# Memory and neighbourhood attention as one stream with dealt-out projections: a hybrid encoder block on 8 cores

## The reference

```python
h = rmsnorm(x) ; parts = h @ w_in                  # 1024 x 11264
# A: three groups of 8 heads of 64 (dilation 1, 4, 16), partial rotary,
#    each query sees keys within 64 steps of its dilated subsequence;
#    the groups are combined by their softmax denominators
# B: 8 heads of 64 on the grid of 32 rows x 64 columns: each query attends
#    8 rows x 16 columns around it (clipped at the edges), with a bias
#    per head and relative position; softmax
# C: 4 heads of 128, cross-attention into rmsnorm(mem) @ w_mem_kv
y = sum(sigmoid(logits_b + bias_b) * ((out_b * silu(g_b)) @ w_branch_b))
x = x + rmsnorm(y @ w_out)
```

## Time and profile before

| | us |
|---|---|
| median of 3 runs | 1269.59 (1269.53 to 1351.25) |
| profiled execution, device time | 1278.77 |
| its span on the slowest core (6) | 1277.2 |
| spans of the eight cores | 1254.3 to 1277.2 |
| stage 0, to A's first q projection | 75.1 |
| A | 75.1 to about 545 |
| C | about 545 to 661 |
| B | 661 to 936.6 (TensorE) |
| merge | 939 to 1206 |
| output | 1206 to 1277 |

### The profile page before, as it was taken

How to read it: one execution, slowest core, us unless ns; L and a number is a source line. 1 busy time by engine, 2 the same in 40 slices (tenths; PEclk the granted TensorE clock), 3 DMA queues, 4 the chain that set the end, 5 groups by cost and what they waited for, 6 DMA issues and landing times.

```text
span 1277.2 us, 21131 instructions; the slowest of 8 cores (1254.3 to 1277.2 us)
## 1 busy us (share of the span) xinstructions
PE 1099.4 (86%) x6768; PEld 539.1 (42%) x6768; DVE 638.6 (50%) x800; ACT 536.5 (42%) x873; POOL 399.6 (31%) x362
## 2 busy tenths in 40 slices
PE   2669999989789988569977899998959999999995
PEld 1535555444344543233344344644424444444442
DVE  3624456557684766844780089107932222222266
ACT  4515554323345432129932465246522222222365
POOL 0113333234454333343320144104532333333300
PEclk9779999989899998789988955895569999999997
DMA  9961204020017434043006410352052000400077
GB/s 228 173 128 15 37 2 51 2 34 1 1 17 68 55 45 51 1 65 78 30 1 81 67 18 2 54 77 35 2 65 34 1 1 1 66 1 1 23 256 266
DMA packets 54988, 68.13 MB, mean 53 GB/s; under 512 B 2272, under 2 KB 46432, under 8 KB 54624
## 3 DMA queue, kind: packets, MB, share of 16 engines
q0 software_dynamic: 44768, 30.41, 19.7%
q1 hardware_dynamic: 10112, 36.36, 9.3%
HBM read 86.81 MB, written 8.39 MB: 75 GB/s over the span
## 4 chain that ended last, share of the span: by engine, by line
PE 64%; DMA 11%; ACT 8%; DVE 7%; issue 7%; POOL 3%; SPq 0%; ACTq 0%; DVEq 0%; POOLq 0%
PE psall L351 26%; PE psall L485 19%; DMA xs<-x 4%; DMA ring<-w_in 3%; PE psall L671 3%; PE psall L724 3%; PE psall L955 3%; PE psall L977 3%; PE psall L544 2%; DVE t L582 2%; ACT pB L964 2%; PE psall L982 1%; DMA wbr<-w_br 1%; PE psall L1021 1%; ACT qb L534 1%
## 5 line engine op out<-in xcount | busy, mean ns | idle before, releaser
L351 PE MATMUL psall<-hT,ring 128*128 128x512 bf16 x1408 | 333.4, 387 | 22.1 <-ACT qcT L866 11.7
L485 PE MATMUL psall<-hT,ring 128*128 128x512 bf16 x896 | 225.6, 393 | 3.0 <-DMA ring<-w_in 3.0
L351 PEld LDWEIGHTS psall<-hT,ring 128*128 128x128 bf16 x1408 | 138.7, 99 | 198.5 <-issue 42.7
L1121 DVE TENSOR_TENSOR tt<-psall,sg 128x512 f32<-128x512 f32 x96 | 66.4, 692 | 202.2 <-ACT sg L1110 173.5
L1110 ACT ACTIVATE sg<-psall,mb_sb 128x512 f32<-128x512 f32 x96 | 66.0, 687 | 196.2 <-PE psall L351 196.2
L485 PEld LDWEIGHTS psall<-hT,ring 128*128 128x128 bf16 x896 | 85.0, 100 | 113.5 <-issue 33.9
L968 DVE TENSOR_TENSOR pn<-pB,ebr 128x384 bf16<-128x384 bf16 (+3 forms) x136 | 61.4, 478 | 141.1 <-ACT pB L964 124.3
L550 POOL TENSOR_TENSOR qT<-t,t 128x512 bf16<-128x512 f32 x48 | 63.6, 1325 | 163.6 <-DVE t L548 162.2
L680 ACT ACTIVATE pA<-psall 128x896 bf16<-128x896 f32 (+1 forms) x80 | 77.8, 972 | 85.5 <-PE psall L671 80.2
L964 ACT ACTIVATE pB<-psall 128x512 bf16<-128x512 f32 (+3 forms) x200 | 85.9, 443 | 55.1 <-PE psall L955 40.1
L534 ACT ACTIVATE qb<-psall 128x512 bf16<-128x512 f32 x96 | 57.5, 599 | 118.1 <-PE psall L485 117.6
(11 more groups left out here) (102 smaller groups left out, 1511.8 us busy)
## 6 DMA issues: line engine op xcount, KB each, us to landing
xs<-x SPq DMA_DIRECT2D x32, 512.0 KB, 5.8
ring<-w_in POOLq DMA_DIRECT2D x28, 512.0 KB, 10.3
ring<-w_in POOLq DMA_DIRECT2D x8, 1024.0 KB, 10.9
out<-on SPq DMA_DIRECT2D x16, 512.0 KB, 3.9
rp<-rpbg SPq DMA_DIRECT2D x8, 448.0 KB, 3.5
wbr<-w_br POOLq DMA_DIRECT2D x6, 512.0 KB, 14.6
ring<-w_mem POOLq DMA_DIRECT2D x2, 1024.0 KB, 10.3
ring<-w_out POOLq DMA_DIRECT2D x2, 1024.0 KB, 14.0
```

Source lines behind the costliest of these rows:

```text
L351: m = pe.matmul(banks[bank_i][0:ncols, 0:n_], lhsT=wv[:, c, col0:col0 + ncols], rhs=r, start=(c == 0), stop=(c == nchunk - 1))
L485: m = pe.matmul(banks[bank][:, cols], lhsT=lhs_fn(c), rhs=rhs_fn(c), start=(c == 0), stop=(c == 7))
L1121: sch.op("dve", lambda e: e.tensor_tensor(out=tts[b][:, :], in0=banks[3 + b][:, :], in1=sgs[b][:, :], op=ALU.mult), reads=[bkey(3 + b), (" ...
```

## The change

- The ring has 10 slots of 128x2048 (`NW` = 10); all pieces are 256 columns wide (w_out: 512 rows by 512 columns), so the ML weights are 12 pieces.
- `zb` and `zc` are laid over `accd` and `accn`; `ebr` (now 23 rows of 64 columns per head), `ropeC`, `ropeS`, `maskA` and `qb` share one buffer `multi`; C's queries sit in 4 pieces of `memT`.
- A: the groups of the second half of the heads go (2, 1, 0) instead of (0, 1, 2). v chunks are interleaved with the q/k jobs. The ropeC product is issued with the projection instead of behind the permute. The reciprocal is cut into two of 256 columns, which wait in a list `dveq` and are issued one at a time behind masks.
- The last window of A has as dense work the memory's keys and values, the first v projection of B, and 5 of 16 half-head steps of the `ebr` tables. Then come the gate of the last head pair, q and k of B's pair 0 and 4 such steps. There is no barrier here; `inherit` hands the waits of old tiles to the new ones.
- B and C are one stream of 16 rounds. A round is one head pair of B with a block of 8 query rows (512 queries) over even key tiles only (`na_blocks`; 6 or 8 key tiles, packed in 5 steps of up to 512 columns per head; `vO` is gone), and 0, 1 or 2 jobs of C. Scores use banks 2 and 3, denominators bank 1, numerators banks 0 and 4 in turn, dense work banks 5 to 7. All products with `ebr` are on VectorE, in place.
- Gates use Tanh instead of Silu (the factor 2 is in the denominators by `twos`) and are stored in `zb` and `zc`.
- `rp` is one buffer of 128x448; a head's table takes two halves, each one DMA, one Exp and three GpSimd products.

```diff
-NW = 6
+NW = 10
+AORD = ((0, 1, 2), (2, 1, 0))
-    ring = [sb("ring%d" % i, [128, 4096], BF16).__enter__() for i in range(NW)]
+    ring = [sb("ring%d" % i, [128, 2048], BF16).__enter__() for i in range(NW)]
...
+        def ebr_half(h, i):
+            def f():
+                old = EOLD[h] + [("ebr", h)]
...
+                sch.dma("sp", out=rp[:, :], in_=rpbg[:, h, 448 * i:448 * i + 448], writes=["rp"], semkey="rp")
+                sch.op("act", lambda e: e.activation(out=rp[:, :], in_=rp[:, :], func=AF.Exp),
+                       reads=["rp"], writes=["rp"])
+                for (o0, n, i0, m) in ((0, 7, 0, 0), (15, 3, 4, 0), (14, 1, 3, 1)) if i == 0 else (
+                        (7, 7, 0, 0), (18, 4, 0, 0), (22, 1, 4, 2)):
+                    sch.op("pool", lambda e: e.tensor_tensor(out=ebr[:, h, o0:o0 + n, :], in0=rv[:, i0:i0 + n, :],
+                                                             in1=cm(m, n), op=ALU.mult),
+                           reads=["rp", "colm"], writes=old)
...
+        def interleave(jobs, extra, lag):
...
+            for n, (ch, late) in enumerate(jobs):
+                out_.append(ch[0])
+                if len(pend) >= lag:
+                    p_ = pend.pop(0)
+                    out_[-1] = (lambda a=ch[0], b=p_: (a(), b()))
+                out_.append(ch[1])
+                pend.append(late)
+                goal = len(extra) * (len(jobs) - n - 1) // len(jobs)
+                while len(extra) > goal:
+                    out_.append(extra.pop(0))
...
+        drain_pv(0)
+        for tb in range(4):
+            for f_ in fin_chunks(1, 1, tb):
+                f_()
+            qkB_chunk(0, 0, tb)()
+            dve_flush(1)
+            qkB_chunk(0, 1, tb)()
+            dve_flush()
+            esteps.pop(0)()
...
+        DENSE = [5, 6, 7]
+        NBS = [0, 4]
...
+        def fin(nbk, z, zkey):
+            dve_flush()
+            i2 = ring_next("t2", 2)
+            t2 = t2s[i2]
+            sch.op("act", lambda e: e.activation(out=t2[:, :], in_=banks[DB][:, :], func=AF.Copy),
+                   reads=[bkey(DB)], writes=[("t2", i2)])
...
+            dveq.extend([rec(0), rec(256), fmul])
...
+        NQK = [2, 2, 2, 2, 2, 2, 2, 2, 3, 1, 1, 3]
+        NVB = [0, 0, 3, 0, 0, 3, 1, 1]
...
+        for gi in range(16):
+            pair, b = gi // 4, gi % 4
+            nC = 2 if gi >= 12 else (0 if gi % 3 == 2 else 1)
+            items = b_items(pair, b)
+            dense = [gate_chunk("B", pair, b)]
+            for c_ in range(nC):
+                h, tb = ccnt // 4, ccnt % 4
+                ccnt += 1
+                dense += [cq_chunk(h, tb), gate_chunk("C", h, tb)]
+                items.append(c_item(h, tb))
+            if gi < 12:
+                dense += [qkb[pair + 1].pop(0) for _ in range(NQK[gi])]
+            if gi < 8:
+                for _ in range(NVB[gi]):
+                    dense += vb1.pop(0)
+            if esteps:
+                n_ = min(4, len(esteps))
+                for k_ in range(n_):
+                    dense.insert(2 * k_ + 1, esteps.pop(0))
+            done = 0
+            for n, item in enumerate(items):
+                drain_pv(1)
+                mask, pv = item()
+                pend_pv.append(pv)
+                goal = (n + 1) * len(dense) // len(items)
+                while done < goal:
+                    dense[done]()
+                    done += 1
+                if mask is not None:
+                    mask()
+                for _ in range(2 if len(dveq) > 2 else 1):
+                    if dveq:
+                        dveq.pop(0)()
+        drain_pv(0)
+        dve_flush()
+        sch.barrier(pe=False)
```

More of the change, by code:

```diff
@@ L271, in add @@
         specs.append((ap, nch))
[L273 to L284, removed]
@@ L677, in s_part @@
[L677 to L680 removed]
+                                m = pe.matmul(banks[SB + h][:, off:off + 64 * n],
+                                              lhsT=kT[h * 64:(h + 1) * 64, 128 * t:128 * t + 128],
+                                              rhs=qT[h * 64:(h + 1) * 64, q0:q0 + 64 * n], start=True, stop=True)
@@ new lines, in item, with c_item, fs, pv @@
+                    return mask, pv
+                items.append(item)
+            return items
+        def c_item(h, tb):
+            nbk = NBS[nfin[0] % 2]
+            nfin[0] += 1
+            def item():
+                ip = ring_next("p", NPB)
+                p = ps[ip]
+                i = (4 * h + tb) % 4
+                def fs(pe):
+                    for mt in range(2):
+                        m = pe.matmul(banks[SB + mt][:, :], lhsT=kmT[:, h, mt * 128:(mt + 1) * 128],
+                                      rhs=qcs[i], start=True, stop=True)
+                    return m
+                sch.op("pe", fs, reads=[("kmT", h // 2), ("qc", i)], writes=[bkey(SB), bkey(SB + 1)])
+                sv = psall[:, SB * 512:(SB + 2) * 512].rearrange("p (h x) -> p h x", h=2)
+                sch.op("act", lambda e: e.activation(out=p[:, :, :], in_=sv, func=AF.Exp, scale=sc_c),
+                       reads=[bkey(SB), bkey(SB + 1)], writes=[("p", ip)])
+                def pv():
+                    def fpv(pe):
+                        for mt in range(2):
+                            pe.matmul(banks[nbk][:, :], lhsT=vm[:, mt, h * 128:(h + 1) * 128], rhs=p[:, mt, :],
+                                      start=(mt == 0), stop=(mt == 1))
+                        for mt in range(2):
+                            m = pe.matmul(banks[DB][:, :], lhsT=twos[:, :], rhs=p[:, mt, :],
+                                          start=(mt == 0), stop=(mt == 1))
+                        return m
+                    sch.op("pe", fpv, reads=[("p", ip), ("vm", 0), ("vm", 1), "twos"], writes=[bkey(nbk), bkey(DB)])
+                    fin(nbk, zc[:, h, 512 * tb:512 * tb + 512], ("zc", h, tb))
+                return None, pv
+            return item
@@ L1129, in build @@
             for b in range(3):
-                wq.release(idx["ML%d%d" % (nh, b)])
+                for i in range(2):
+                    wq.release(idx["ML%d%d%d" % (nh, b, i)])
         sch.barrier(pe=False)
-    if debug:
-        sch.dma("sp", out=dbg["yT"][:, :, :], in_=yT[:, :, :], semkey="dbg")
-        sch.barrier()
     with ExitStack() as es_:
```

1130 lines of the change are left out of this document (515 added, 615 removed).

## The result

The changed kernel takes 1295.8 us, median of 4 runs (1291.6 to 1297.6), beside 1269.6 for the kernel before: ratio 1.020, 95% interval 1.017 to 1.023. It is slower by 1.7 to 2.3%, where 1178 was forecast, 7% faster. Some executions of a version show a lower clock on one die and are longer; every time given here is the median of the others. Profiled execution: 1297.6 us, slowest core's span 1295.1.

What follows compares the result with a forecast made beforehand. It took TensorE, busy 86% of the span, as the bound, with its waits and slow clock to be cut; stage terms summed to 1186.4 us, divided by 1.0072 to 1178, range 1125 to 1230.

Steps and rivals of the forecast that it cites:

- start of A: A's first projection, behind stage 0's barrier: four more ring DMAs add 15 us to 75.1, giving 90.1.
- A's windows 0 to 10: A's first eleven windows: fewer waits and less slow clock save 31 us (bounds 15 to 45), 430 becomes 399.
- last window: A's last window: memory keys and values, B's first v projection, gate chunks and attention steps take 36 us.
- tail: Behind A's last window: 12 projection chunks and four bias-table halves, 24 us instead of 21.
- stream: The 16 merged rounds of B and C: 239 us of engine work, 21 of turns, 20 of bias tables, 280.
- from its end to the last instruction: Last barrier and merge stage, behind the stream: 340.7 becomes 356 us (bounds 346 and 370).
- taking the larger engine in each round: Stream: 12 rounds bound by TensorE or even, 166 us, and four by VectorE, 73 us; sum 239.
- 21 us for turns: Stream: addition for turns between engines, from A's TensorE busy share of 89% at 0.96; bounds 5 and 60.
- the handovers cost more: Rival, stream: late masks stop the other engine, 0.5 us more per item; 1225 typical, 1238 at most; chance 20%.
- The bias chain: Bias tables built through one `rp` buffer, 6 us a half: 20 us more in the stream (bounds 0 and 40).
- The interleaving: A's first eleven windows: v projections among q/k have `qb` ready, saving some 12 of 18.1 us of waits.
- Slow clock: Rival: attention pulls the whole stream to 1.2 GHz, its 227 us becoming 454, some 1371 in all; chance 5%.

Runs made afterwards that it cites:

- e5: Changed kernel with the 64 half reciprocals of the stream left out, the multiply kept: 1214.8 us, ratio 0.956.
- e15: Changed kernel without the stream's reciprocals, with two `rp` buffers loaded ahead and six ring pieces issued before stage 0's barrier: 1185.2 us, ratio 0.934.
- e1: Changed kernel with both reciprocals and the multiply of an output issued at once with its PV: 1305.6 us, ratio 1.028.
- e7: Changed kernel with the stream's PV put off by two items instead of one: 1260.9 us, ratio 0.993.
- e13: Changed kernel with two-item lag, two `rp` buffers, six ring pieces before the barrier, masks ahead of projections, reciprocals at once: 1231.2 us, ratio 0.968.
- e16: As e13, with three numerator banks and two for dense work instead of two and three: 1240.3 us, ratio 0.975.
- e14: Kernel before the change, with the reciprocals of memory and neighbourhood attention replaced by copies: 1251.9 us, ratio 0.984.
- e2: Changed kernel without the loads and Exps of the seven bias-table halves in the stream: 1266.4 us, ratio 0.996.
- e4: Changed kernel with six ring pieces issued before stage 0's barrier and the other four behind it: 1277.5 us, ratio 1.005.
- e10: Changed kernel with the v projections of A's first eleven windows ahead of q/k again: 1297.9 us, ratio 1.022.
- e6: Changed kernel with an item's mask multiplies issued before its projections and gate multiplies: 1281.8 us, ratio 1.009.
- e3: Changed kernel with a second `rp` buffer, each table load issued one step ahead: 1281.5 us, ratio 1.009.

## Why the prediction was wrong

The sum, term by term, on the profiled execution (core 3), in us:

| term | forecast | measured |
|---|---|---|
| start of A | 90.1 | 92.1 |
| A's windows 0 to 10 | 399 | 416.3 |
| last window | 36 | 44.0 |
| tail | 24 | 23.6 |
| stream | 280 | 365.5 |
| from its end to the last instruction | 355.7 | 353.7 |
| around the span | 1.6 | 2.5 |
| sum | 1186.4 | 1297.6 |

**The failed step** is "taking the larger engine in each round", with 21 us for turns. The sizes of its parts were right: VectorE 217 us forecast, 214.6 measured; a reciprocal 1.75 and 1.75 us; TensorE's work 227 forecast, 238 to 239 where little stops it (e5, e15). But the maximum of two engines is reached only if neither waits for the other, and here each item makes a loop, scores, Exp, mask, PV, with one item of slack: 2.9 us by the forecast's own 280 us over 96 items (3.8 as measured, with the waits in it). A pair of reciprocals, 3.5 us in VectorE's in-order queue, is longer than that, whether it stands behind the projections or right behind its PV (e1), and the queue's head idles for the tanh of a gate meanwhile. Without the reciprocals the stream is 80 us shorter (e5); with them, one more item of slack brings 33 (e7). What the other 47 are made of stays open: with a lag of two, masks first and reciprocals at once the stream still is 44.5 us longer than without reciprocals (e13 333.4, e15 288.9), though VectorE is busy 69% of e13's.

Two premises of that step were misread. It let "a 1.75 us reciprocal" stand in front of a mask, where the loop issues both halves in a row. And it took A, "busy 89% at 0.96 with the same scheme", as its check. A's scheme is another: its halves go one at a time (but for two pairs) and its masks ahead of half of the projections, and it has reciprocals only where its gates are, in the changed kernel eight pairs from 308 to 388:

```profile
308.00:388.00 80.00, 67.48 (x446) 35.46 (x445) 60.09 (x65) 27.84 (x40) 39.80 (x32) 0.91 0.14 19
```

There VectorE is busy 75%, more than in the stream, with a pair every 10 us as there, and TensorE, busy 84% at 0.91, waits for it 0.4 us (its longest row is 7.3 us for `kT`, by GpSimd). So reciprocals as dense as the stream's can be hidden; whether dealing out the halves would do it in the stream is the rival that no run tested.

**The rival "the handovers cost more"** named the mechanism, a late mask stopping the other engine, but at 0.5 us an item its price, 48 us, was too low, and I let two numerator banks speak against it. They did not prevent it; nor does a third bank, taken from dense work, help on top of e13's lag (e16). A third bank in the changed kernel itself was not tried. The rival gave 1225 as typical and 1238 as its far end, so my range, which took its top from it, ended 66 us too low. The stream's 365.5 us are also past the 320 that I had named as a sign of being wrong.

**What the old kernel hid.** I counted reciprocals as work in both forms, and never asked what stood over them before. In C it was ScalarE (with 30 table loads, 15 of them at L882), in B TensorE at 0.50. Both covers went: 85 us of this work cost the old stages 20 (e14), 112 cost the stream 80 (e5).

**The bias chain**, priced at 20 in the stream (bounds 0 and 40), is 23 (e2), and its place was as told: Exp waiting on the DMA of `rp`. The price within was different: of the 38.1 us that ScalarE waited, 14.9 are one wait, for a load that took 11.3 us where every load was taken at the 3.1 of `colm`.

**Start of A**, +15: right, +17.0 in the trace and 16.1 taken back by e4. That is 4.0 to 4.3 us for each of four pieces, against the 3.5 of the earlier trace rows. The fit in the Trainium skill, "DMA: Bandwidth & Descriptors", section "Anatomy of one DMA", gives 4.4 us for 1 MB; an estimate by it puts the start at 92.7, and the trace has 92.1.

**A's windows**, 31 saved forecast, 13.7 measured. The interleaving was taken as 12 and is 2.4 (e10): `qb` is late with it too, 12.9 us in 14 waits, and `kT` rose from 8.6 to 11.6. The `accd` waits fell from 22.2 us to 7.4 in the whole of A, where the forecast had most of them gone. **Last window**: TensorE's 36 us of work measured 36.2, but three waits on `accd` (1.7, 1.7 and 3.3 us, at the hand-over from one query block to the next) and small ones came on top. Both were read from the trace, not tried; no run takes these waits away.

**Right**: no table load in the stream (the changed kernel has 4 in all, 30 before in C alone); the wait in the middle of the merge stage, 5.28 us for 5.6; `wbr` in use 16.9 us behind the last attention work, against 12.5 and "about 6 more". **Slow clock**: the stream's 0.86 went with the waits (0.95 in e5, 0.97 in e15), so what I wrote against that rival stands. The rule weighed ahead of the run, in "TensorE: Matmul & The Clock Gate", section "Part 1: The HAM clock gate" of the Trainium skill, is that the clock is set by how busy TensorE is; e15 (busy 86%, clock 0.97) and the old stretch (93%, 0.50) can't both follow from it. What decides between them no run here settles.

**Scaling**: I divided by 1.0072, as the profiled execution before stood so to its median; after it is 1.0014, so 7 us of the miss of 118 are there. For a kernel of 8 cores the slowest core of one execution is no constant.

## What to carry to other kernels

Before two stages are merged to fill each other's gaps, list what each long instruction of the support engines was hidden behind, and ask whether that cover stays. In a merged stream the time is not the larger of two engines: for every loop between them compare its slack in time with the longest thing that can stand in its queue, here 2.9 us an item against a pair of reciprocals of 3.5. That comparison is my account of e1, e6 and e7, not a measured threshold. Where the slack is the smaller, one more item of lag was the cheapest help here (33 us, against 15 for the order of the masks and a loss for the order of the reciprocals). Small loads that an in-order engine waits for are better issued well before bulk DMAs (one step ahead brought half, e3), and bulk DMAs behind a barrier, not ahead of it (e4).

## What the runs showed of the hardware

- A 224 KB load, 2.5 us at the least and 3.2 in the middle of its kind, took 11.3 us while six 512 KB ring pieces issued on another queue were in flight, in a stretch with a DMA share of 0.53. The forecast had taken 3.1 for each.
- TensorE's granted clock did not follow its busy share alone: 0.50 at 93% in the earlier trace rows, 0.60 at 97% in e14, 0.97 at 86% in e15. Fewer waits came with a higher clock: the same stream's matmuls were busy 268.7 us at 0.86 and 237.9 us at 0.97, so that of the 88 us between these two streams 31 are slower matmuls and 57 are waits.
- A reciprocal of 256 columns takes 1748 ns, a gate multiply of 512 columns 682 ns: 5.1 times as much a column, from PSUM and from SBUF alike. The Trainium skill, "VectorE: DVE Perf Modes", section "First, the fixed hardware budget", says that a reciprocal repeats its divide steps with a count of 8; the rows have 6.8 ns a column against 1.3. The same denominator stands in 64 or 128 rows; whether it can be laid out so that a reciprocal has fewer columns was not tried.
